# Zero-padded queries, a mask folded into the contraction, and one sliding-window unit per tile in a hybrid attention encoder

## The chip, the cores and the metric

The kernel runs on one core of a Trainium2 chip. The time is the device time of one launch in microseconds, and the figure compared is the median of several runs. The profile shows one execution, instruction by instruction, on the core's engines: TensorE (PE, with its weight loads as PEld), VectorE (DVE), ScalarE (ACT), GpSimd (POOL), and SyncE (SP), which only issues DMAs here.

## The reference

Two layers of a streaming encoder. Each layer normalises its input (1024 prompt frames, and 16 new frames of 8 running streams), projects it, and feeds three groups of heads, all in float32:

```
A  forgetting attention: 4 heads x 64, causal per frame,
   logit[t,s] += sum of log f_j over s < j <= t
B  latent attention: 8 heads, key = 64 columns out of a latent + 32 rotary columns,
   mask: key chunk <= query chunk (chunks of 64 frames)
C  sliding window: 4 query heads on 2 key heads x 64, own chunk and the 2 before,
   a bias by relative position, a learned sink per head
x = x + concat(A, B, C) @ W_out;  x = x + MLP(RMSNorm(x))
```

Each group is softmax(scale * q k^T + bias or mask) v. The mask of B adds -1e30 where the key's chunk lies behind the query's.

## The kernel before

The layer runs in stages: projection of the input, preparation of latents and keys, attention of the prompt, attention of the streams, output projection, MLP. The prompt has 8 tiles of 128 queries. For each tile the work is cut into *units*: the two steps of the latent query's projection (`q1`, `q2`), then units of heads of one kind (`fox`, `swa` for sliding, `mla` for latent). `tile_units` (line 99) decides how many heads share a unit: as many as fit in 1024 score columns, except `swa`, which has two. So a tile has two `swa` units; `mla` has one unit of eight heads in tile 0, two of four in tile 1, four of two in tiles 2 and 3, and eight of one in tiles 4 to 7. The order in a tile is q1, two fox units, q2, the other fox units, the swa units, the mla units; in the last tile the streams' q1 and q2 are put in by position from the end of that list.

All engines walk the same list of units, each with its own lag. For unit i, TensorE transposes the probabilities of unit i-3 (`probs_transposes`, line 2164), computes the scores of unit i (`scores`, lines 2134 and 2136) and the value product of the heads that end with unit i-4 (`values`, line 2187). VectorE copies transposed probabilities of unit i-3 (line 1620), normalises unit i-2 (1629, 1632), takes the maxima of unit i (1657 for mla; 1664 with the bias table for the others) and copies out the heads of i-4 (1681). ScalarE copies its share of the transposed probabilities (1217) and then takes the exponentials of unit i (1234, 1238).

The transposes come in *chunks* of up to four 128 x 128 blocks, each chunk into one of two PSUM banks. Chunks are numbered through the layer: even numbers go to bank 4 and are copied by VectorE, odd ones to bank 5 and are copied by ScalarE.

```
            for g in range(heads):
                h, s0 = h0 + g, score_column(kind, t, g)
                if kind == "fox":
                    rows = slice(64 * (h % 2), 64 * (h % 2) + 64)
                    q, keys, mask = qkTf[rows, h // 2, toks[t]], qkTf[rows, 2 + h // 2, :], cmaskB
                elif kind == "swa":
                    rows = slice(64 * (h // 2), 64 * (h // 2) + 64)
                    q, keys, mask = qkTs[rows, h % 2, toks[t]], qkTs[rows, 2, :], None
                else:
                    q, keys, mask = qTm[t % 2][:, h, :], kTm[:, h, :], mmaskB
```

FoX and sliding heads lie two and two on the 128 partitions, 64 rows each, so their scores contract over 64 rows; a latent head has 96 rows of its own. A score in float32 is two instructions per 512 columns. The masks of fox and mla are added by one more matmul per head, the identity times a bf16 mask, onto the last 128 columns. SP's queue loads, in order, the latent weights, the bias and band tables (line 622 for all loads), and stores new cache entries and finished heads (`mix_d`). GpSimd does nothing during the attention.

Of the kernel before, what the change touches and what calls it, by code (L numbers as in the profile page):

```python
# [21 lines left out]
P = 128  # L22
# [10 lines left out]
QK_M = HD + ROPE  # L33
FF = 4 * D
# [167 lines left out]
def hybrid_step(nc, a, c, o):  # L202

    (y_p, y_s, fk_p, fv_p, lf_p, ckv_p, kr_p, sk_p, sv_p, fk_s, fv_s, lf_s, ckv_s, kr_s, sk_s, sv_s) = o
    with ExitStack() as ctx:
# [35 lines left out]
        mmaskB = keep("mmaskB", [P, P], BF16)  # L241
# [82 lines left out]
        kTm = at("kTm", HT, [QK_M, MLA_H, NPT * P])  # L324
# [14 lines left out]
        qTm = [at(f"qTm{i}", RING + 24576 + i * 4096, [QK_M, MLA_H, P]) for i in range(2)]  # L339
# [4 lines left out]
        triL = at("triL", RING + 48640, [P, P])  # L344

# [37 lines left out]
        constB = at("constB", Z + 512, [P, P])  # L383
# [19 lines left out]
        pro_pe = signal("prologue_pe", 0)  # L403
        pro_dve = signal("prologue_dve", 0)
# [19 lines left out]
        tables_in = signal("wukv_bias_in", 16 * 3)  # L424
# [20 lines left out]
        max_done = signal("max_done", NATTN)  # L445
        has_waited = signal("dve_has_waited", 0)
# [11 lines left out]
        st_prep = signal("stream_rotary_queries", 1)  # L458
        st_rest = signal("stream_queries_and_gates", 1)
# [160 lines left out]
        def _(sp):  # L620
# [4 lines left out]
            for dst, src in ((identF, c["ident"]), (constA, c["cmask"]), (constB, c["mmask"]), (onehot, c["onehot"]),  # L625
# [9 lines left out]
            for l in range(DEPTH):  # L635
# [36 lines left out]
                load(wukv[:].rearrange("p h e d -> p (h e d)"), a["w_ukv"][l], tables_in)  # L672

# [237 lines left out]
        def _(pool):  # L911
# [7 lines left out]
            for l in range(DEPTH):  # L919
# [32 lines left out]
                for t in range(NPT):  # L952
                    if t >= 2:
# [3 lines left out]
                                            ALU.mult).then_inc(lb_ok.sem, 1)  # L957
                for i in range(PC_IN, MLP0):
                    lo(i, i % NSLOT, 1024)
# [107 lines left out]
        def _(act):  # L1067

            act.wait_ge(const_in.sem, 16 * 5)
            nc.scalar.copy(identB[:], identF[:])  # L1070
            nc.scalar.copy(cmaskB[:], constA[:])
            nc.scalar.copy(mmaskB[:], constB[:]).then_inc(pro.sem, 1)
            act.wait_ge(pro_pe.sem, 1)
# [9 lines left out]
            for l in range(DEPTH):  # L1083
# [125 lines left out]
                for i in range(len(UNITS) + LAG):  # L1209
# [8 lines left out]
                    if i < len(UNITS):  # L1218
# [6 lines left out]
                        elif kind == "q2":  # L1225
                            act.wait_ge(sc_mm.sem, sc_mm.at(l, i + 1))
                            nc.scalar.copy(qTm[t % 2][:], S[0:QK_M, :].rearrange("p (h n) -> p h n", h=MLA_H)
# [1360 lines left out]
```

## Time and profile before

| | |
|---|---|
| median of 3 runs | 2941.55 us (2939.71 to 2943.75) |
| the profiled execution | 2936.66 us, its span 2934.9 us |
| mean granted TensorE clock | 0.981 of full speed |
| busy over the span | PE 95%, DVE 61%, ACT 37%, POOL 35% |

The span runs from the first to the last instruction. Busy time of TensorE is modelled from starts, so a busy engine need not be at its peak: what one instruction costs is read from the starts of the next ones.

### The profile page before, as it was taken

The page shows a single profiled execution, that of the slowest core. Times are in us where ns is not written, and L with a number is a line of the kernel's source. Part 1 is how long each engine was busy: PE and PEld are TensorE (multiplying, and loading weights), DVE is VectorE, ACT ScalarE, POOL GpSimd, SP SyncE. Part 2 cuts the span into 40 slices and gives each one's busy share as a digit, 9 for nine tenths or more (in the row PEclk, how much of TensorE's full clock was granted, in tenths as well). Part 3 has the DMA queues.
Part 4 walks back from the last instruction along what each step waited for, and adds up shares of the span by engine and source line. Part 5 has one row for each costly group of instructions (what it writes and reads, how often), then busy time and mean ns, then how long its engine had stood idle before and what let it go on. Part 6 is the DMA issues. An engine that isn't in the chain of part 4 may idle for free.

```text
span 2934.9 us, 40047 instructions
## 1 busy us (share of the span) xinstructions
PE 2787.1 (95%) x15094; PEld 2228.3 (76%) x15094; DVE 1777.0 (61%) x2533; ACT 1076.4 (37%) x1894; POOL 1023.7 (35%) x501
## 2 busy tenths in 40 slices
PE   7999999899999999999999999998899999999995
PEld 5985666678788887888789666667778888788884
DVE  3126777733644649888730477775256564788884
ACT  3224544433332333333332355443243323333333
POOL 2110000012644456777511100000145444567765
PEclk9999999999999999999999989999999999999997
DMA  5210000532334346343131100013323433654331
GB/s 203 62 55 14 23 8 25 156 122 79 126 111 150 142 163 250 131 144 128 59 114 55 47 15 15 16 46 127 129 93 133 150 131 123 256 174 139 129 118 72
DMA packets 164389, 310.68 MB, mean 106 GB/s; under 512 B 24704, under 2 KB 89504, under 8 KB 164256
## 3 DMA queue, kind: packets, MB, share of 16 engines
q1 hardware_dynamic: 159936, 301.82, 29.7%
q10 hardware_dynamic: 4320, 7.08, 0.7%
q8 instruction: 85, 1.39, 0.2%
q14 instruction: 48, 0.39, 0.0%
HBM read 206.42 MB, written 102.44 MB: 105 GB/s over the span
## 4 chain that ended last, share of the span: by engine, by line
PE 84%; DVE 7%; issue 3%; ACT 2%; POOL 2%; DMA 1%; ACTq 0%; SPq 0%; DVEq 0%; POOLq 0%
PE ps L2458 7%; PE ps L2462 7%; PE ps L2460 7%; PE ps L2134 7%; PE ps L2368 7%; PE ps L2369 6%; PE ps L2370 6%; PE ps L1990 5%; PE ps L1988 5%; PE ps L1989 5%; PE ps L2164 4%; PE ps L2187 4%; PE ps L2249 1%; PE ps L2106 1%; PE ps L2318 1%
## 5 line engine op out<-in xcount | busy, mean ns | idle before, releaser
L935 POOL TENSOR_TENSOR w_lo<-w_raw,w_hi 128x1024 fp32r<-128x1024 f32 (+2 forms) x32 | 70.0, 2192 | 1034.3 <-ACT w_hi L1091 1034.3
L2458 PE MATMUL ps<-wq_hi,sa_hi 128*128 128x512 f32 x896 | 350.2, 391 | 5.2 <-DVE x L1921 5.2
L2460 PE MATMUL ps<-wq_lo,sa_hi 128*128 128x512 f32 x896 | 349.8, 390 | 0.0
L2462 PE MATMUL ps<-wq_hi,sa_lo 128*128 128x512 f32 x896 | 349.8, 390 | 0.0
L1921 DVE TENSOR_TENSOR x<-ps,x 128x1024 f32<-128x1024 f32 x224 | 264.2, 1212 | 56.4 <-PE ps L2462 51.7
L1859 DVE TENSOR_TENSOR sa_lo<-ra,sa_hi 128x1024 fp32r<-128x1024 f32 x112 | 280.8, 2509 | 23.9 <-ACT sa_hi L1353 23.9
L975 POOL TENSOR_TENSOR wq_lo<-wsum,wq_hi 128x1024 fp32r<-128x1024 f32 x64 | 157.3, 2459 | 291.0 <-ACT wq_hi L1333 291.0
L1988 PE MATMUL ps<-w_hi,hT_hi 128*128 128x512 f32 (+2 forms) x672 | 248.5, 370 | 0.1
L1990 PE MATMUL ps<-w_hi,hT_lo 128*128 128x512 f32 (+2 forms) x672 | 246.2, 366 | 0.0
L1989 PE MATMUL ps<-w_lo,hT_hi 128*128 128x512 f32 (+2 forms) x672 | 245.1, 365 | 0.0
L1851 DVE TENSOR_TENSOR cq<-ps,cq 128x1024 f32<-128x1024 f32 x48 | 58.7, 1222 | 286.4 <-ACT cq L1394 244.2
L981 POOL TENSOR_TENSOR wq_lo<-bsum,wq_hi 128x1024 fp32r<-128x1024 f32 x64 | 171.2, 2686 | 114.7 <-ACT wq_hi L1344 114.7
L2368 PE MATMUL ps<-hT_hi,wq_hi 128*128 128x512 f32 x512 | 202.1, 395 | 6.8 <-DVE hT_lo L1815 6.8
L981 POOL TENSOR_TENSOR wq_lo<-rq,wq_hi 128x1024 fp32r<-128x1024 f32 x64 | 168.6, 2644 | 96.9 <-ACT wq_hi L1344 96.9
L2458 PEld LDWEIGHTS ps<-wq_hi,sa_hi 128*128 128x128 f32 x896 | 169.0, 189 | 42.0 <-issue 6.0
L2370 PE MATMUL ps<-hT_hi,wq_lo 128*128 128x512 f32 x512 | 200.1, 391 | 0.0
L2369 PE MATMUL ps<-hT_lo,wq_hi 128*128 128x512 f32 x512 | 200.1, 391 | 0.0
L2462 PEld LDWEIGHTS ps<-wq_hi,sa_lo 128*128 128x128 f32 x896 | 168.9, 189 | 35.4
L2460 PEld LDWEIGHTS ps<-wq_lo,sa_hi 128*128 128x128 f32 x896 | 168.9, 189 | 34.6
L975 POOL TENSOR_TENSOR wq_lo<-rq,wq_hi 128x1024 fp32r<-128x1024 f32 x64 | 170.5, 2674 | 57.8 <-ACT wq_hi L1333 57.3
L1394 ACT COPY cq<-ps 128x512 f32<-128x512 f32 x128 | 73.3, 587 | 277.7 <-PE ps L2370 161.3
L2164 PE MATMUL ps<-identF,pbuf 128*128 128x128 f32 x984 | 143.8, 283 | 22.2 <-DVE pbuf L1632 14.3
(317 smaller groups left out, 6377.5 us busy)
## 6 DMA issues: line engine op xcount, KB each, us to landing
ra<-hidden_scratch SPq DMA_DIRECT2D x112, 512.0 KB, 3.3
hidden_scratch<-cq SPq DMA_DIRECT2D x94, 512.0 KB, 2.7
rq<-in_w_up_dram SPq DMA_DIRECT2D x64, 512.0 KB, 3.8
rq<-in_w_down_dram SPq DMA_DIRECT2D x64, 512.0 KB, 4.3
residual_scratch<-x SPq DMA_DIRECT2D x36, 512.0 KB, 5.1
x<-residual_scratch SPq DMA_DIRECT2D x36, 512.0 KB, 6.6
w_raw<-in_w_in_dram SPq DMA_DIRECT2D x16, 512.0 KB, 4.9
mixer_scratch<-omixT SPq DMA_DIRECT2D x16, 512.0 KB, 2.6
```

The lines of the kernel that those rows point to most:

```text
L975: nc.gpsimd.tensor_tensor(wq_lo[o % 4][:], up_source(o)[:], wq_hi[o % 4][:], ALU.subtract).then_inc(up_lo.sem, 1)
L981: nc.gpsimd.tensor_tensor(wq_lo[k][:], down_b_source(o)[:], wq_hi[k][:], ALU.subtract).then_inc(b_lo.sem, 1)
L1859: nc.vector.tensor_tensor(low.rearrange("p k n -> p (k n)"), raws, high.rearrange("p k n -> p (k n)"), ALU.subtract).then_inc(a_lo.sem, 1)
L1988: pe.matmul(out, ah, bh, start=(k == 0), stop=False)
L1989: pe.matmul(out, ah, bl, start=False, stop=False)
L1990: last = pe.matmul(out, al, bh, start=False, stop=(k == n - 1))
L2368: pe.matmul(out, wh[:, cols], h[:, k, :], start=new and k == 0, stop=False, skip_group_check=True)
L2369: pe.matmul(out, wh[:, cols], lo_h[:, k, :], start=False, stop=False, skip_group_check=True)
L2370: last = pe.matmul(out, wl[:, cols], h[:, k, :], start=False, stop=k == 3, skip_group_check=True)
L2458: pe.matmul(out, ah[:, k, :], bh[:, k * 512:(k + 1) * 512], start=new and k == 0, stop=False, skip_group_check=True)
L2460: pe.matmul(out, ah[:, k, :], bl[:, k * 512:(k + 1) * 512], start=False, stop=False, skip_group_check=True)
L2462: last = pe.matmul(out, al[:, k, :], bh[:, k * 512:(k + 1) * 512], start=False, stop=final and k == 1, skip_group_check=True)
```

## The change

The FoX and sliding queries of a tile are copied by GpSimd into buffers of 128 rows (`qzf`, `qzs`), whose other 64 rows hold zeros, and the scores contract over all 128 rows of the keys. The latent mask becomes eight more contraction rows of `qTm` and `kTm`: row b of the keys is 1 where the key lies in the second chunk of block b, row t of the queries is -1e30 for the first chunk's queries of tile t. SP loads these rows, the keys' once and the queries' per tile. The four sliding heads of a tile form one unit. Several prologue semaphores are merged on the way.

```diff
+QK_X = QK_M + 8
 def tile_units(kind, t):
-    n = 2 if kind == "swa" else min(HEADS[kind], 1024 // head_stride(kind, t))
+    n = min(HEADS[kind], 1024 // head_stride(kind, t))
...
+def scores_behind(kind, t):
+    return max(u for u, unit in enumerate(UNITS) if unit[0] == kind and unit[1] == t) + 1
...
-        kTm = at("kTm", HT, [QK_M, MLA_H, NPT * P])
+        kTm = at("kTm", HT, [QK_X, MLA_H, NPT * P])
+        qzf = [at(f"qzf{i}", (RING + 47104, HT + 71296)[i], [P, FOX_H, P]) for i in range(2)]
+        qzs = [at(f"qzs{i}", NRM + 8192 + i * 2048, [P, SWA_H, P]) for i in range(2)]
...
                 load(wukv[:].rearrange("p h e d -> p (h e d)"), a["w_ukv"][l], tables_in)
+                load(kTm[QK_M:QK_X], c["mask_mla_k"].unsqueeze(1).broadcast_to([NPT, MLA_H, NPT * P]), tables_in)
+                def query_mask(t):
+                    load(qTm[t % 2][QK_M:QK_X], c["mask_mla_q"][t].unsqueeze(1).broadcast_to([NPT, MLA_H, P]), qmask_in)
+                query_mask(0)
+                sp.wait_ge(qmask_in.sem, qmask_in.at(l, 16))
+                query_mask(1)
...
                 for t in range(NPT - 1):
                     sp.wait_ge(o_ev.sem, o_ev.at(l, TILE_END[t]))
                     load(mix_d[t], omixT[t % 2][:].rearrange("p k n -> p (k n)"), mix_out[t % 2])
+                    if t + 2 < NPT:
+                        sp.wait_ge(qmask_in.sem, qmask_in.at(l, 16 * (t + 2)))
+                        query_mask(t + 2)
...
+                def pad_zeros(bufs, other):
+                    for buf in bufs:
+                        for r in range(2):
+                            nc.gpsimd.memset(buf[64 * r:64 * r + 64, other(1 - r), :], 0.0)
+                def pad_queries(dst, src, planes, t):
+                    for r in range(2):
+                        rows = slice(64 * r, 64 * r + 64)
+                        last = nc.gpsimd.tensor_copy(dst[t % 2][rows, planes(r), :], src[rows, 0:2, toks[t]])
+                    last.then_inc(qz_ok.sem, 1)
...
+                pool.wait_ge(nb_mm.sem, nb_mm.at(l, NPT))
+                pool.wait_ge(lat_ok.sem, lat_ok.at(l, NT))
+                pad_zeros(qzf, fox_planes)
+                pool.wait_ge(stg_ev.sem, stg_ev.at(l, 2 * NT))
+                pad_queries(qzf, qkTf, fox_planes, 0)
+                pad_queries(qzf, qkTf, fox_planes, 1)
+                pool.wait_ge(lat_ev.sem, lat_ev.at(l, NT))
+                pool.wait_ge(prep_out.sem, prep_out.at(l, 16 * 10))
+                pad_zeros(qzs, swa_planes)
+                pad_queries(qzs, qkTs, swa_planes, 0)
+                pad_queries(qzs, qkTs, swa_planes, 1)
+                for t in range(2, NPT):
+                    pool.wait_ge(sc_mm.sem, sc_mm.at(l, scores_behind("fox", t - 2)))
+                    pad_queries(qzf, qkTf, fox_planes, t)
+                    pool.wait_ge(sc_mm.sem, sc_mm.at(l, scores_behind("swa", t - 2)))
+                    pad_queries(qzs, qkTs, swa_planes, t)
...
                     if kind == "mla" and h0 == 0:
+                        pe.wait_ge(qmask_in.sem, qmask_in.at(l, 16 * (t + 1)))
                         pe.wait_ge(sm_done.sem, sm_done.at(l, UNITS.index(("q2", t, 0, 0)) + 1))
+                    if kind == "fox" and h0 == 0:
+                        pe.wait_ge(qz_ok.sem, qz_ok.at(l, t + 1 if t < 2 else 2 * t + 1))
+                    if kind == "swa" and h0 == 0:
+                        pe.wait_ge(qz_ok.sem, qz_ok.at(l, t + 3 if t < 2 else 2 * t + 2))
...
-                            rows = slice(64 * (h % 2), 64 * (h % 2) + 64)
-                            q, keys, mask = qkTf[rows, h // 2, toks[t]], qkTf[rows, 2 + h // 2, :], cmaskB
+                            q, keys, mask = qzf[t % 2][:, h, :], qkTf[:, 2 + h // 2, :], cmaskB
...
-                            rows = slice(64 * (h // 2), 64 * (h // 2) + 64)
-                            q, keys, mask = qkTs[rows, h % 2, toks[t]], qkTs[rows, 2, :], None
+                            q, keys, mask = qzs[t % 2][:, h, :], qkTs[:, 2, :], None
...
-                            q, keys, mask = qTm[t % 2][:, h, :], kTm[:, h, :], mmaskB
+                            q, keys, mask = qTm[t % 2][:, h, :], kTm[:, h, :], None
```

## Rows read from the trace of the kernel before

**Rows 1.** Stretches of the first attention: us, busy us per engine (instructions), PEclk, DMA share, GB/s.
```profile
342.00:384.20 42.20, 40.69 (x311) 27.92 (x309) 32.60 (x104) 21.47 (x51) 0.00 (x0) 1.00 0.04 14
...
sum 324.00, PE 309.53 PEld 208.61 DVE 234.68 ACT 154.87 POOL 0.00; mean PE 34.39 PEld 23.18 DVE 26.08 ACT 17.21 POOL 0.00
```

**Rows 2.** TensorE's longest waits in the same stage: us, times, longest.
```profile
PE ps L2164 <- DVE pbuf L1632: 7.6, 10, 2.1
```

**Rows 3.** Timeline of TensorE, tile 5: start, us, operation, [idle <-releaser].
```profile
396.82 0.88 PE L2164 MATMUL ps<-identF,pbuf 128*128 128x128 f32 x6
397.63 1.55 PE L2134 MATMUL ps<-qkTf 64*128 64x512 f32 x4
399.12 0.23 PE L2136 MATMUL ps<-cmaskB,identB 128*128 128x128 bf16 x1
...
406.67 0.85 PE L2164 MATMUL ps<-identF,pbuf 128*128 128x128 f32 x6 [0.63 <-ACT ptb L1217]
...
423.80 0.87 PE L2164 MATMUL ps<-identF,pbuf 128*128 128x128 f32 x6
424.51 1.46 PE L2134 MATMUL ps<-kTm,qTm 96*128 96x512 f32 x4
425.80 0.22 PE L2136 MATMUL ps<-mmaskB,identB 128*128 128x128 bf16 x1
425.91 0.88 PE L2164 MATMUL ps<-identF,pbuf 128*128 128x128 f32 x6
```

**Rows 4.** Timeline of TensorE, tile 2, inside a latent unit.
```profile
303.46 0.22 PE L2136 MATMUL ps<-mmaskB,identB 128*128 128x128 bf16 x1
303.51 0.86 PE L2134 MATMUL ps<-kTm,qTm 96*128 96x384 f32 x2
```

**Rows 5.** Groups by line and form, first layer's attention: copies of transposed probabilities.
```profile
L1620 DVE COPY ptb<-ps 128x512 f32<-128x512 f32 x27 | 18.6, 690 | 4.5 <-PE ps L2164 4.3
...
L1620 DVE COPY ptb<-ps 128x256 f32<-128x256 f32 x19 | 8.0, 422 | 2.3 <-PE ps L2164 2.0
...
L1620 DVE COPY ptb<-ps 128x384 f32<-128x384 f32 x12 | 6.7, 557 | 2.4 <-PE ps L2164 2.2
...
L1620 DVE COPY ptb<-ps 128x128 f32<-128x128 f32 x12 | 3.5, 290 | 1.4 <-PE ps L2164 1.2
...
L1217 ACT COPY ptb<-ps 128x512 f32<-128x512 f32 x68 | 39.0, 574 | 3.7 <-PE ps L2164 3.6
```

**Rows 6.** Timeline of VectorE, a latent step of tile 4.
```profile
377.48 0.82 DVE L1657 TENSOR_REDUCE mx<-ps 128x1 f32<-128x640 f32 x1 [0.19 <-PE ps L2136]
```

**Rows 7.** Timeline of VectorE, maxima of a sliding unit, tile 5.
```profile
403.67 0.48 DVE L1664 CUSTOM_DVE_ANT_0 pbuf<-ps,bias,sink_bc 128x256 f32<-128x256 f32 x1
...
404.07 0.48 DVE L1664 CUSTOM_DVE_ANT_0 pbuf<-ps,bias,sink_bc 128x256 f32<-128x256 f32 x1
```

**Rows 8.** Timeline of ScalarE, the same sliding unit and the copy behind it.
```profile
405.47 0.49 ACT L1238 ACTIVATE pbuf<-pbuf,negm 128x256 f32<-128x256 f32 x1
...
405.96 0.56 ACT L1217 COPY ptb<-ps 128x512 f32<-128x512 f32 x1
```

**Rows 9.** Timeline of the preparation: VectorE with GpSimd idle, and beside it.
```profile
205.25 0.34 DVE L1578 SCALAR_TENSOR_TENSOR zc<-zc,lat_rs,gkv_bc 128x128 f32<-128x128 f32 x1
...
213.92 1.16 POOL L955 TENSOR_TENSOR lb<-logf,minus 128x512 f32<-128x512 f32 x1 [0.29 <-PE ps L2073]
214.10 1.12 DVE L1578 SCALAR_TENSOR_TENSOR zc<-zc,lat_rs,gkv_bc 128x128 f32<-128x128 f32 x1
```

**Rows 10.** Timeline of the preparation: the band's load, first key product, bias sum.
```profile
210.71 0.51 SPq L622 DMA_DIRECT2D band<-const_band_dram  x1
...
226.75 7.48 PE L2084 MATMUL ps<-latT,wukv 128*64 128x512 f32 x32 [0.81 <-DVE latT L1588]
...
241.09 1.22 DVE L1608 TENSOR_TENSOR bias<-bias,band 128x1024 f32<-128x1024 f32 x1
```

**Rows 11.** DMA issues from 195 to 245 us: KB, median us to landing.
```profile
band<-const_band_dram SPq DMA_DIRECT2D x1, 128.0 KB, 5.9
```

More of the change, by code:

```diff
@@ L338, in hybrid_step @@
         wukv = at("wukv", RING + 20480, [P, MLA_H, 2, HD])
-        qTm = [at(f"qTm{i}", RING + 24576 + i * 4096, [QK_M, MLA_H, P]) for i in range(2)]
+        qTm = [at(f"qTm{i}", RING + 24576 + i * 4096, [QK_X, MLA_H, P]) for i in range(2)]
         omixT = [at(f"omixT{i}", RING + 32768 + i * 4096, [P, KC, P]) for i in range(2)]
@@ L423, in hybrid_step @@
         gains_in = signal("latent_gains_in", 16 * 4)
-        tables_in = signal("wukv_bias_in", 16 * 3)
+        tables_in = signal("wukv_bias_in", 16 * 4)
+        qmask_in = signal("mla_query_mask_in", 16 * NPT)
         prep_out = signal("prep_out", 16 * 10)
@@ L445, in hybrid_step @@
         max_done = signal("max_done", NATTN)
+        qz_ok = signal("padded_queries_copied", 2 * NPT)
         has_waited = signal("dve_has_waited", 0)
@@ L622, in load @@
                 sp.dma_start(dst, src).then_inc(sem.sem, 16)
-            for dst, src in ((identF, c["ident"]), (constA, c["cmask"]), (constB, c["mmask"]), (onehot, c["onehot"]),
+            for dst, src in ((identF, c["ident"]), (constA, c["cmask"]), (onehot, c["onehot"]),
                              (relb, a["rel_bias"])):
@@ L1067, in _ @@
         def _(act):
-            act.wait_ge(const_in.sem, 16 * 5)
+            act.wait_ge(const_in.sem, 16 * 4)
             nc.scalar.copy(identB[:], identF[:])
-            nc.scalar.copy(cmaskB[:], constA[:])
-            nc.scalar.copy(mmaskB[:], constB[:]).then_inc(pro.sem, 1)
-            act.wait_ge(pro_pe.sem, 1)
+            nc.scalar.copy(cmaskB[:], constA[:]).then_inc(pro.sem, 1)
+            act.wait_ge(pro_tab.sem, 2)
             nc.scalar.mul(skew[:], ps[:, 0:2048].rearrange("p (h n) -> p h n", h=SWA_H)[:, :, 0:384],
@@ L1226, in _ @@
                             act.wait_ge(sc_mm.sem, sc_mm.at(l, i + 1))
-                            nc.scalar.copy(qTm[t % 2][:], S[0:QK_M, :].rearrange("p (h n) -> p h n", h=MLA_H)
+                            nc.scalar.copy(qTm[t % 2][0:QK_M], S[0:QK_M, :].rearrange("p (h n) -> p h n", h=MLA_H)
                                            ).then_inc(sm_done.sem, 1)
@@ L1251, in _ @@
                     if i == 1:
[L1252 removed]
+                        act.wait_ge(st_q.sem, st_q.at(l, 1))
                     if i == FIRST["fox"]:
@@ L1716, in prepare @@
                         if i == 7:
-                            last.then_inc(st_rest.sem, 1)
+                            last.then_inc(st_q.sem, 1)
                 dve.wait_ge(ql_mm.sem, ql_mm.at(l, 1))
@@ L1977, in _ @@
         def _(pe):
-            pe.wait_ge(pro_dve.sem, 1)
+            pe.wait_ge(pro_tab.sem, 1)
             for h in range(SWA_H):
                 last = pe.matmul(bank(h)[:, 0:384], relbb[:, h, :], onehot[:], start=True, stop=True)
-            last.then_inc(pro_pe.sem, 1)
+            last.then_inc(pro_tab.sem, 1)
             pe.wait_ge(pro.sem, 1)
@@ L2540, in shape_constants @@
     tables["cmask"] = np.where(col <= row, f32(0), neg)
-    tables["mmask"] = np.where(col // chunk <= row // chunk, f32(0), neg)
+    block = np.arange(NPT)[:, None]
+    key = np.arange(NPT * P)[None, :]
+    tables["mask_mla_k"] = ((key // P == block) & (key % P >= chunk)).astype(f32)
+    mask_q = np.zeros((NPT, NPT, P), f32)
+    for t in range(NPT):
+        mask_q[t, t, 0:chunk] = neg
+    tables["mask_mla_q"] = mask_q
     lag = (row // chunk + 2) - np.arange(2 * P)[None, :] // chunk
```

23 lines of the change are left out of this document (11 added, 12 removed).

## The prediction

> **What bounds the kernel now.** The change lives in one stage, the prompt attention of each layer, so I read that stage before the whole. The table of stretches [rows 1] is first: in the first layer's attention TensorE is busy 309.53 of 324.0 us, VectorE 234.68, ScalarE 154.87, GpSimd not at all. The reader is to see that two engines are close to full: in the fifth query tile (342 to 384.2 us) VectorE has 32.60 of 42.2 us. The table of waits comes next [rows 2]: TensorE's largest wait on another engine in the whole stage is 7.6 us. So TensorE sets the pace, and a nanosecond taken from it counts until VectorE or ScalarE becomes late.
>
> But "busy" does not say what TensorE is busy with. The timeline of one tile, read by the starts of successive lines, does [rows 3]. From the first of six transposes to the score that follows takes 0.71 us before a latent score with 96 contraction rows (423.80 to 424.51) and 0.81 us before a FoX score with 64 (396.82 to 397.63). Both scores have 768 keys, yet from score to mask it is 1.29 us with 96 rows (424.51 to 425.80) and 1.49 with 64 (397.63 to 399.12). The array pays for going from 128 rows to 64 and back: 0.10 us going in, and 0.20 us for the unhidden second weight load and the way out. Between 96 and 128 rows nothing of the kind appears.
>
> **The change part by part.** Durations are of one profiled execution, 2936.66 us with a span of 2934.9; the median of the runs shown is 2941.55, so 4.9 us go on top at the end.
>
> *FoX queries padded to 128 rows.* Each head's score then costs what the latent one costs. 4 heads, 8 tiles, 2 layers: 64 x (0.10 + 0.20) = 19.2 us off TensorE. The padding itself adds nothing there, since the 96-row score of the same width shows no cost per row.
>
> The rows show the four 64-row passes of a FoX head running one after the other, 1.49 us for what 96 rows do in 1.29. The Trainium skill ("TensorE: Matmul & The Clock Gate", Why this matters for your kernels) says that matmuls of few contraction rows, placed in different row groups, run concurrently; that rule speaks against padding, which occupies the whole array. By the rule up to half of the score time would be within reach of a 64-row kernel; by the rows, this kernel gets none of it, as a mask stands between heads of opposite halves, so nothing is lost.
>
> *Sliding queries padded.* 32 units now enter and leave 64-row mode. I take the same 0.10 going in and 0.10 behind the first pass, and leave out the exit, often followed by another switch: 32 x 0.20 = 6.4 us.
>
> *Four sliding heads as one unit.* One value product of 64 output columns per tile goes, 16 in all. Its two switches are not in the rows; I price them like the FoX ones, 0.10 each: 3.2 us.
>
> *Latent mask as contraction rows.* 8 heads, 8 tiles, 2 layers: 128 mask matmuls go. One costs 0.05 us where another score follows (303.46 to 303.51) [rows 4] and 0.11 where transposes follow (425.80 to 425.91) [rows 3]. I take 0.08: 10.2 us. Eight more rows in the score cost nothing, by the 96-row argument.
>
> Gross sum: 19.2 + 6.4 + 3.2 + 10.2 = 39.0 us.
>
> *What VectorE and ScalarE take back.* Here the diff does something that it does not say. Copies of transposed probabilities go by chunk number, even ones to VectorE, odd ones to ScalarE. The first tile has 1 + 1 + 1 + 2 = 5 chunks before, and 1 + 1 + 2 = 4 after, since the merged sliding unit has 4 blocks in one chunk. Every later unit has two chunks (the sliding pair together two as well), so the parity turns over for the whole rest of the layer. Before, ScalarE had the full chunks (68 of 512 columns) and VectorE the remainders: 12 of 128, 19 of 256 and 12 of 384 columns [rows 5]. After, VectorE gets the full ones: per layer 12 x (0.69 - 0.29) + 18 x (0.69 - 0.42) + 12 x (0.69 - 0.56) = 11.2 us more, in tiles 2, 4, 5 and 6 (one of the 19 is the first tile's). The merged unit gives it back some 0.6 us a tile of small operations.
>
> In the latent steps of those four tiles VectorE has almost no room: in tile 4 it waits 0.19 us for the scores per step [rows 6], and the copy grows by 0.40. So there the mask's gain is void: half of 10.2 = 5.1 us back. In tile 4 the excess is 0.40 - 0.19, say 0.15 us on 8 steps, in tile 2 0.2 us on 4 steps: (1.2 + 0.8) x 2 = 4.0 us back.
>
> The merged unit also makes a longer link. Its maxima take 4 x 0.40 us on VectorE [rows 7], its exponentials 4 x 0.49 us on ScalarE, and only then does ScalarE copy (0.56 us) the transposed chunk that frees the bank [rows 8]: 1.6 + 0.35 + 2.0 + 0.2 + 0.56 = 4.7 us after the scores. TensorE meanwhile has a value block (1.3 us), six transposes (0.7) and a latent score (1.3), 3.3 us. That is up to 1.4 us of stall, and the normalisation of four heads adds one in the next step; before there was a stall of 0.63 us on the same copy [rows 3] and one like it after. I take 0.45 us a tile: 16 x 0.45 = 7.2 us back. For FoX I take back 15%, 2.9 us, for steps that have no value product between two normalisations.
>
> *GpSimd's padding copies.* 16 calls a layer with two copies each; those of tiles 0 and 1 run ahead of the stage, where GpSimd has nothing else to do, and 24 a layer within it, two tiles ahead of their use, so TensorE never waits for them. Behind GpSimd's own waits stand only later copies and the low halves of the output weights, wanted after the stage. What they can do is hold VectorE: an operation with both inputs in SBUF takes 0.34 us with GpSimd idle and 1.12 us while a GpSimd product of 512 columns (1.16 us) runs [rows 9]. Bounds for one copy: 0 if no such operation meets it, 0.55 if it always does (256 columns, half of 1.16). Normalisations are about a quarter of VectorE's time, and half of a delay there should reach the end: 48 x 0.25 x 0.55 x 0.5 = 3.3 us back.
>
> *Loads.* SP's queue now has the key mask, the first query mask and a wait for its landing ahead of the bias and band tables. The band was issued at 210.71 us [rows 10] and took 5.9 us to land [rows 11], so about 216.6; TensorE waits for the tables only at 226.75. A landing plus two more issues shift it by some 4 to 6 us: hidden by 10.1 us. Behind it stand the prep stores, for whose end VectorE waits before the bias sum at 241.09 us [rows 10], and GpSimd before padding the sliding queries; both have over 10 us to spare. Later query masks are issued behind the mixer stores, a tile and more ahead. The dropped constant is far from the path, and in the last tile the first projection of the streams' queries now stands before the last FoX head in place of after it, with two units still between it and its second step. All this I cost at nothing; if the cover failed, each microsecond would show twice, once a layer.
>
> Net: 39.0 - 5.1 - 4.0 - 7.2 - 2.9 - 3.3 = 16.5 us, so 2936.7 - 16.5 = 2920.2 us, and 2925 on the scale of the median. By the bounds alone it lies between 39 us less (2902) and nothing.
>
> **The rivals.** *All of it comes through.* The lags of two to four units absorb the longer sliding unit and VectorE's copies; for it speaks the 27% of VectorE idle over the stage. Gain 30 to 39 us: 2902 to 2911. *VectorE becomes the bound.* The 22.4 us of copies reach the end in full and the merged unit's stall is its full 1 us a tile: 39.0 - 10.2 - 22.4 - 16 + 9 (what VectorE's own idle time and lighter unit cover) is about 0: 2936 to 2946. *GpSimd blocks VectorE, slower.* Every one of the 48 copies holds a normalisation as the row shows, 0.78 us (1.12 - 0.34), at places where VectorE binds: 37 us in place of 3.3, a loss of 17, about 2959. It decides from 19.8 / 48 = 0.41 us a copy on the path. Against it: a copy has half of that row's columns, and VectorE mostly reads PSUM here. The Trainium skill ("SBUF — State Buffer", Who interferes with whom) says that VectorE and GpSimd share a port pair as an exclusive lock, held for the whole instruction, and that scalings like these normalisations can need it too; the row of 1.12 us agrees, for an operation with two SBUF inputs only. *The change doesn't do what it says.* The 0.30 us per FoX head comes from something else than the row count, such as the two sources of the queries, and stays: 39.0 - 19.2 - 6.4 = 13.4 against 5.1 + 4.0 + 7.2 + 3.3 = 19.6 taken back, 6 us slower, about 2948. Against it, the 96-row scores of the same tile.
>
> **How the numbers follow.** My forecast, a net gain of 8 to 27 us (2914 to 2933): 0.56. All through: 0.17. VectorE the bound: 0.14. GpSimd: 0.07. Not as it says: 0.06. 0.2% is 5.9 us, about what a measurement here tells from no change. Faster, below 2935.7: 0.56 + 0.17 and a little of the third, 0.75. Same: most of the third, 0.13. Slower: 0.12. The range leaves out the fastest few and the slower tail: 2904 to 2939; the likeliest case's own is 2914 to 2933.
>
> **What the profile after would show.** FoX and sliding scores with 128 rows, 0.71 us after six transposes, 1.29 us to the mask at 768 keys; no latent mask; VectorE's copies all of 512 columns, ScalarE's the short ones; a longer TensorE wait two or three steps after each sliding unit, behind ScalarE's copy or VectorE's normalisation; GpSimd copies of 256 columns two tiles ahead. I am wrong if TensorE's waits in the stage stay near 10 us a layer (then it is the first rival), if they grow past 30 (the second), or if VectorE's normalisations lengthen during GpSimd's copies (the third).

## The result, and the profile after

The changed kernel takes 2906.72 us (median of 4 runs, 2904.44 to 2910.41); in the same session the kernel before takes 2940.63 (4 runs, 2939.63 to 2943.75). The ratio is 0.9884, 95% interval 0.9867 to 0.9901: some 34 us faster, where 16.5 were forecast. The profiled execution takes 2906.52 us, its span 2904.7, with a mean granted clock of 0.984 (0.981 before). Between the two profiled executions lie 30.1 us, since that of before was 4 us below its median.

The table of stretches of the changed kernel, cut at the tiles of the first layer's prompt attention, is the first view, with columns as in [rows 1]. A tile's length here always runs from the start of the last instruction of the last latent score of one tile to that of the next; the first tile starts with the last product of its `q1`.

```profile
245.22:254.62 9.40, 6.04 (x50) 5.33 (x48) 5.82 (x31) 5.45 (x16) 1.58 (x4) 1.00 0.00 0
254.62:275.16 20.54, 17.64 (x106) 13.31 (x105) 14.48 (x54) 11.08 (x44) 1.58 (x4) 0.92 0.07 27
275.16:303.37 28.21, 25.82 (x191) 17.92 (x190) 24.19 (x80) 15.95 (x52) 1.58 (x4) 1.00 0.06 22
303.37:332.44 29.07, 28.72 (x199) 18.32 (x198) 23.90 (x73) 14.71 (x42) 1.58 (x4) 1.00 0.06 21
332.44:374.57 42.13, 39.77 (x310) 27.96 (x309) 35.39 (x100) 19.77 (x53) 1.58 (x4) 1.00 0.04 15
374.57:417.02 42.45, 40.86 (x304) 28.13 (x302) 35.70 (x94) 18.89 (x49) 1.69 (x4) 1.00 0.04 14
...
sum 274.94, PE 258.23 PEld 177.59 DVE 219.96 ACT 133.24 POOL 9.61; mean PE 32.28 PEld 22.20 DVE 27.49 ACT 16.65 POOL 1.20
```

VectorE has 35.39 of 42.13 us in tile 4, and 35.70 of 42.45 in tile 5. The column to look at next is PEclk: 1.00 in the first tile and 0.92 in the second. The same view of the kernel before, for the first two tiles of the first layer and then of the second:

```profile
244.40:257.04 12.64, 10.20 (x57) 7.87 (x56) 6.62 (x37) 6.57 (x21) 0.00 (x0) 0.85 0.01 1
257.04:280.58 23.54, 22.66 (x133) 15.75 (x133) 16.75 (x65) 12.05 (x47) 0.00 (x0) 0.87 0.06 23
1686.97:1701.01 14.04, 12.87 (x57) 9.97 (x56) 6.69 (x37) 6.57 (x21) 0.00 (x0) 0.61 0.00 0
1701.01:1724.45 23.44, 22.57 (x133) 15.72 (x133) 16.75 (x65) 12.03 (x47) 0.00 (x0) 0.87 0.06 23
```

Before, TensorE was granted 1.2 GHz in place of 2.4 for parts of both tiles, in both layers. [Rows 1] show a stretch at 1.00, and the prediction has no term for the clock.

TensorE's waits in the first layer's attention after the change, largest first:

```profile
PE ps L2218 <- DVE pbuf L1683: 13.7, 19, 2.3
...
PE ps L2218 <- ACT ptb L1268: 0.9, 3, 0.3
```

The wait for VectorE's normalisation grew from 7.6 us [rows 2] to 13.7; that for ScalarE's copy shrank to 0.9, from this in the kernel before:

```profile
PE ps L2164 <- ACT ptb L1217: 3.8, 8, 0.8
```

The groups of copies of transposed probabilities show why (VectorE, then ScalarE):

```profile
L1671 DVE COPY ptb<-ps 128x512 f32<-128x512 f32 x70 | 48.1, 687 | 6.3 <-PE ps L2218 6.0
L1268 ACT COPY ptb<-ps 128x512 f32<-128x512 f32 x28 | 16.2, 578 | 1.7 <-PE ps L2218 1.5
L1268 ACT COPY ptb<-ps 128x256 f32<-128x256 f32 x18 | 6.5, 361 | 1.1 <-PE ps L2218 1.0
L1268 ACT COPY ptb<-ps 128x384 f32<-128x384 f32 x12 | 5.6, 467 | 0.2 <-PE ps L2218 0.2
L1268 ACT COPY ptb<-ps 128x128 f32<-128x128 f32 x12 | 3.1, 254 | 0.7 <-PE ps L2218 0.7
```

Against [rows 5] the engines have changed places, as the prediction read out of the chunk numbers. Last, TensorE's timeline of tile 5, FoX and then the steps behind the merged sliding unit:

```profile
387.37 0.88 PE L2218 MATMUL ps<-identF,pbuf 128*128 128x128 f32 x6
388.08 1.46 PE L2188 MATMUL ps<-qkTf,qzf 128*128 128x512 f32 x4
389.37 0.22 PE L2190 MATMUL ps<-cmaskB,identB 128*128 128x128 bf16 x1
...
397.31 0.66 PE L2218 MATMUL ps<-identF,pbuf 128*128 128x128 f32 x4 [0.22 <-DVE pbuf L1683]
398.26 0.44 PE L2218 MATMUL ps<-identF,pbuf 128*128 128x128 f32 x2 [0.29 <-ACT ptb L1268]
...
400.44 1.09 PE L2218 MATMUL ps<-identF,pbuf 128*128 128x128 f32 x8 [0.45 <-DVE pbuf L1683]
```

A FoX score starts 0.71 us after six transposes and its mask 1.29 us later; in [rows 3] that was 0.81 and 1.49. Behind the sliding unit TensorE waits 0.22 + 0.29 + 0.45 = 0.96 us.

### The profile page after: what moved, and what is told of

The parts are those of the page before. It is cut to its first block, busy times and chain, and to the rows that moved or that the text cites. A ratio compares the mean times of both kernels' runs of the same rounds, so it can differ in the third digit from the quotient of the medians.

```text
span 2904.7 us, 39773 instructions
## 1 busy us (share of the span) xinstructions
PE 2745.5 (95%) x14966; PEld 2216.3 (76%) x14966; DVE 1781.9 (61%) x2451; ACT 1056.3 (36%) x1877; POOL 1054.7 (36%) x581
## 4 chain that ended last, share of the span: by engine, by line
PE 83%; DVE 9%; issue 3%; ACT 2%; POOL 2%; DMA 1%; ACTq 0%; DVEq 0%; SPq 0%; POOLq 0%
PE ps L2512 7%; PE ps L2516 7%; PE ps L2514 7%; PE ps L2422 7%; PE ps L2423 7%; PE ps L2424 7%; PE ps L2041 5%; PE ps L2039 5%; PE ps L2040 5%; PE ps L2188 5%; PE ps L2218 4%; PE ps L2241 3%; PE ps L2303 2%; PE ps L2372 1%; PE ps L2157 1%
```

## The experiments

Every run below is timed in 5 rounds beside the kernel before, whose medians were 2938.89 (first two sessions) and 2939.95 (third). This table has the tile lengths (us) of the first layer in each trace; on the right stand how long TensorE was granted 1.2 GHz in the prompt attention of layer 1 and of layer 2, how long the two attentions are together, and the median. The median belongs to the whole kernel, and the clock also falls in stages that no edit here touches; the column of the attentions leaves those out.

```
tile                    0     1     2     3     4     5     6     7   1.2 GHz   both   median
before              12.64 23.54 28.36 32.66 42.44 43.66 48.43 57.63  10.2 17.1  580.4  2940.6
masks alone         12.54 22.98 27.84 32.32 42.18 43.37 48.13 57.34  13.6 13.6  573.9  2932.7
padding alone       12.42 23.34 27.61 31.39 41.27 42.61 47.18 56.24  10.2  3.4  562.2  2923.1
padding + masks      9.85 22.10 27.24 31.04 41.01 42.32 46.89 55.94   3.4  3.4  553.2  2907.6
 same, parity turned 9.85 21.01 28.09 30.34 41.78 43.03 46.57 55.30   0.0  0.0  552.3  2908.9
merged unit alone    9.93 20.36 28.00 30.59 42.94 43.42 47.44 59.13   6.8  6.8  563.0  2922.9
 same, old parity    9.93 20.98 28.16 31.11 45.29 44.75 49.53 59.79  23.8 20.4  578.5  2935.6
after                9.40 20.54 28.21 29.07 42.13 42.45 46.32 56.82   3.4  3.4  549.8  2906.7
 same, old parity    9.41 20.70 28.39 29.52 42.15 42.84 47.27 58.97   6.8  3.4  556.5  2918.2
 copies x3           9.92 20.97 28.40 29.46 42.36 42.99 46.34 58.17   6.8 13.6  559.3  2914.0
before, filled      13.55 25.34 28.35 32.66 42.44 43.66 48.42 57.63  13.6  3.4  580.2  2936.0
after, filled        9.41 18.93 28.23 29.08 42.14 42.46 46.32 58.09   3.4  3.4  549.3  2904.2
after, some merged   9.40 20.54 28.76 28.63 42.22 42.45 46.32 55.30   3.4  3.4  547.2  2901.5
 some merged, filled 9.40 18.93 28.76 28.62 42.21 42.44 46.32 55.30   0.0  0.0  544.0  2900.6
```

My theory on seeing the result was that the padding's gain came through and that something in tiles 0, 1 and 3 had added to it; the rivals were the clock, the merged unit, and the turned parity.

**Padding alone.** The changed kernel with two sliding units and the latent mask as a matmul.

```diff
-    n = min(HEADS[kind], 1024 // head_stride(kind, t))
+    n = 2 if kind == "swa" else min(HEADS[kind], 1024 // head_stride(kind, t))
-q, keys, mask = qTm[t % 2][:, h, :], kTm[:, h, :], None
+q, keys, mask = qTm[t % 2][:, h, :], kTm[:, h, :], mmaskB
...
```

> The kernel before with the FoX and sliding queries padded to 128 rows alone; latent mask matmuls and two-head sliding units stay, so the chunk parity stays too. Theory A (the gain is the switches between 64 and 128 rows): 64 x 0.30 + 32 x 0.20 = 25.6 us off TensorE, VectorE has room, 20 to 26 us less than before, and the low clock in tiles 0 and 1 stays as before. Theory B (a good part of the measured 34 us is TensorE's clock staying up in tiles 0 and 1, brought by the padding): also the 6.8 and 13.7 us at 1.2 GHz in tile 0 are gone, 26 to 33 us less. Theory C (the 0.30 us do not come from the row count): under 8 us less.

Measured 2923.1 (2920.17 to 2923.98), ratio 0.9946 (0.9932 to 0.9959): 15.8 us faster, less than Theory A's 20 to 26 and B's 26 to 33, and more than Theory C's 8. By the table, tiles 2 to 7 gain 6.88 us, and 6.91 in the second layer: 13.8 / 12 = 1.15 us a tile, 18.4 for sixteen.

**Masks alone.** The changed kernel with two sliding units and the 64-row queries of before.

```diff
-q, keys, mask = qzf[t % 2][:, h, :], qkTf[:, 2 + h // 2, :], cmaskB
+rows = slice(64 * (h % 2), 64 * (h % 2) + 64)
+q, keys, mask = qkTf[rows, h // 2, toks[t]], qkTf[rows, 2 + h // 2, :], cmaskB
...
```

> The kernel before with the latent mask as contraction rows alone. Theory A: 128 x 0.08 = 10.2 us off TensorE and, with the old chunk parity, VectorE can follow: 6 to 10 us less. My prediction's view, that VectorE keeps half of it: 3 to 6 us less. Theory B (clock): more than 10 us less only if tile 0 stays at 2.4 GHz here.

Measured 2932.68 (2930.08 to 2937.55), ratio 0.998 (0.9971 to 0.9989): 6.2 us, where Theory A begins and the prediction's view ends. Tiles 3 to 7 gain 0.26 to 0.34 us each and tile 2 gains 0.52: 2.00 us for 48 heads, 0.04 a head. Theory B's condition didn't come: the stretches at 1.2 GHz are together as long as before.

**Merged unit alone.** The kernel before with one line of the diff. The parity turns over with it.

```diff
-    n = 2 if kind == "swa" else min(HEADS[kind], 1024 // head_stride(kind, t))
+    n = min(HEADS[kind], 1024 // head_stride(kind, t))
```

> The kernel before with four sliding heads in one unit alone, still 64 rows and with the latent mask; the chunk parity turns over. My prediction's terms: 3.2 less for 16 value blocks, 16 x 0.45 = 7.2 more for the longer unit, 4 to 11 more for VectorE's copies of 512 columns: 5 to 15 us slower. The rival, that the merged unit removes waits where it stood instead of adding them (tiles 0, 1 and 3 of the changed kernel are 3 to 5 us shorter each): 5 to 15 us faster. Theory B would show as tile 0 at 2.4 GHz.

Measured 2922.92 (2918.14 to 2925.5), ratio 0.9949 (0.9935 to 0.9962): 16 us faster, a little past the rival's number and far from mine. The part that the prediction charged most to is worth as much alone as the padding. The table shows two places: tiles 0 and 1, where the stretches at 1.2 GHz shrink, and tiles 3 and 6.

**Padding and masks, two sliding units.** The first line of the first diff alone.

> The changed kernel with two-head sliding units again: padding and mask rows, old chunk parity. Theory A: the two parts add, 25.6 + 6 to 10: 28 to 34 us less than before, and the difference to the changed kernel is what the merged unit and the parity are worth together. My prediction's view of the merged unit (7.2 + 4.0 back, 3.2 gained) would put this kernel 5 to 8 us below the changed one; the rival view, that merging helps, puts it 3 to 10 us above.

Measured 2907.6 (2906.57 to 2907.99), ratio 0.9893 (0.9878 to 0.9908): 31.3 us, where the two parts alone give 15.8 + 6.2. Of this surplus of 9.3 us the two attentions hold 2.6 (27.2 us less, where the parts give 18.1 and 6.5): tiles 2 to 7 add up (the masks give 1.86 us on top of the padding, and 2.00 alone), but the first layer's tile 0, which shrank by 0.2 and 0.1 us under each part, shrinks by 2.8 under both together, as the 1.2 GHz stretch in it is gone. The rest lies outside the attention, where the execution with the masks alone has 9.8 us more at 1.2 GHz than the kernel before, and this one 3.4 less. The changed kernel, with the merged unit on top, stands 0.9 us below by the medians, and its attentions are 3.4 us shorter.

**The changed kernel with the old parity.** The first tile's merged unit goes in two chunks of two blocks, so every later chunk keeps its engine of before.

```diff
+def chunk_blocks(u):
+    return 2 if UNITS[u][0] == "swa" and UNITS[u][1] == 0 else 4
-        _chunks += (len(key_blocks(_u)) * UNITS[_u][3] + 3) // 4
+        _chunks += -(-len(key_blocks(_u)) * UNITS[_u][3] // chunk_blocks(_u))
...
```

> The changed kernel, but the first tile's merged sliding unit is cut into two chunks of two blocks, so that the chunk numbers of every later unit have the parity of the kernel before: ScalarE copies the full chunks of 512 columns again, VectorE the short remainders. Theory A (the prediction's: VectorE's 11.2 us of extra copies per layer cost time in the tiles where a VectorE step is tight): tiles 2 and 4, which gained 0.25 and 0.0 us under the change, gain about 1 us each per layer, and the whole is 3 to 6 us faster than the changed kernel. Theory B (parity is worth the same either way, the lags of two to four units absorb it; what counts is the merged unit itself): within 2 us of the changed kernel's 2906.7. Theory C (the merged unit is late in ScalarE's exponentials, and taking copies off ScalarE is what made the merge pay, as in tile 3, which gained 3.7 us): 3 to 8 us slower than the changed kernel, and tile 3 loses about 2 us per layer.

Measured 2918.16 (2912.34 to 2921.01), ratio 0.9927 (0.9915 to 0.994): 11 us slower than the changed kernel. That is Theory C's direction, but past its 3 to 8, and tile 3 loses 0.45 us, not 2. With a merged unit the prediction's price for the parity has the wrong sign. Tile 5 shows the wait: with the old parity TensorE (first row) stands behind ScalarE's copy (second row), which comes after the four exponentials:

```profile
399.62 0.85 PE L2225 MATMUL ps<-identF,pbuf 128*128 128x128 f32 x6 [1.47 <-ACT ptb L1275]
...
398.92 0.56 ACT L1275 COPY ptb<-ps 128x512 f32<-128x512 f32 x1
```

In the changed kernel VectorE copies the full chunk while ScalarE is still at its exponentials, and ScalarE the short one behind them:

```profile
395.86 0.68 DVE L1671 COPY ptb<-ps 128x512 f32<-128x512 f32 x1
...
397.86 0.35 ACT L1268 COPY ptb<-ps 128x256 f32<-128x256 f32 x1
```

TensorE then starts its first four transposes 0.22 us late and waits 0.29 us for the other two, in place of 1.47 for all six. Not all of the 11 us is this wait: the two attentions are 6.7 us longer, and outside them the stretches at 1.2 GHz add up to 103.9 us in this profiled execution, against 83.6 in the changed kernel's.

**The merged unit alone, with the old parity.** The same edit on the kernel before.

> The kernel before with the four sliding heads as one unit and nothing else of the change, but with the first tile's merged unit in two chunks, so that ScalarE keeps the full chunks as before. It stands beside the run with the merged unit alone (2922.9, chunk parity turned over). Theory A (the turned parity, which the prediction priced as a loss of 4.0 us, is a gain, because it takes the 512-column copy off ScalarE just when ScalarE has four exponentials of 0.49 us to do): 5 to 11 us slower than the merged unit alone, 2928 to 2934. Theory B (the prediction's: VectorE's full copies cost, so keeping the old parity is better): 2 to 5 us faster than it, 2918 to 2921. Theory C (in heads of 64 rows the parity makes no difference): within 2 us.

Measured 2935.63 (2928.94 to 2943.23), ratio 0.9987 (0.9978 to 0.9997): 4.3 us faster than the kernel before. Theory A, with 12.7 us a little past its range. With the parity turned the unit alone saved 16.0 us, so about three quarters of that went with the old parity. How much of it is the copy's wait and how much the clock is not separated: the two attentions have 44.2 us at 1.2 GHz, against 13.6 with the parity turned. Its tile 4 shows the cost, on TensorE's timeline and then in the table of stretches:

```profile
362.68 1.30 PE L2171 MATMUL ps<-identF,pbuf 128*128 128x128 f32 x5 [2.46 <-ACT ptb L1224]
```

```profile
355.00:362.00 7.00, 5.22 (x43) 3.45 (x41) 5.87 (x25) 4.41 (x15) 0.00 (x0) 1.00 0.00 1
362.00:369.00 7.00, 6.32 (x20) 4.65 (x21) 3.65 (x12) 3.27 (x8) 0.00 (x0) 0.51 0.01 2
```

A wait of 2.46 us behind ScalarE's copy, and from 362.1 us, within it, the granted clock is 1.2 GHz for 6.8 us. So this stall cost its own length, and the work behind it was slower as well.

**Parity turned, two sliding units.** Padding and masks, with the first tile's FoX unit cut in two chunks.

```diff
+def chunk_blocks(u):
+    return 2 if UNITS[u][0] == "fox" and UNITS[u][1] == 0 else 4
...
```

> The changed kernel with two sliding units of two heads, as in the run with padding and mask (2907.6), but with the first tile's FoX unit in two chunks of two blocks, so that the parity of every later chunk is turned over and VectorE copies the full chunks. Theory A (the turned parity pays only with four sliding exponentials in a row): within 2 us of 2907.6. Theory B (it pays by itself, as ScalarE's share of the copies is the late one in any case): 3 to 6 us faster, 2902 to 2905. Theory C (the prediction's: VectorE is the tight engine in tiles 2, 4, 5 and 6): 2 to 5 us slower, 2910 to 2913.

Measured 2908.9 (2905.59 to 2910.85), ratio 0.9902 (0.9887 to 0.9917): Theory A, 1.3 us from the run without the turn. Inside it two things nearly cancel: tiles 2, 4 and 5 lose 0.85, 0.77 and 0.71 us, and tiles 3, 6 and 7 gain 0.70, 0.32 and 0.64; tile 1 gains 1.1 with the 3.4 us at 1.2 GHz gone.

**GpSimd's copies three times over.** In tiles 2 to 7, so 96 more copies in all.

```diff
-                    for r in range(2):
-                        rows = slice(64 * r, 64 * r + 64)
-                        last = nc.gpsimd.tensor_copy(...)
+                    for j in range(3 if t >= 2 else 1):
+                        if j:
+                            pool.wait_ge(qz_ok.sem, qz_ok.at(l, copied[0]))
+                        for r in range(2): ...
```

> The changed kernel with each of GpSimd's padding copies for tiles 2 to 7 issued three times over: 48 copies become 144 in the attention of the two layers. Theory A (the prediction's price, 0.07 us a copy for holding VectorE): 96 more copies, 6.6 us slower than the changed kernel's 2906.7. Theory B (the copies cost nothing, since VectorE reads PSUM in most of its work and no normalisation lengthened beside a copy): within 1.5 us. The third rival of the prediction (0.78 us a copy): 75 us slower.

Measured 2913.98 (2910.88 to 2915.25), ratio 0.9912 (0.9898 to 0.9926): 7.3 us slower than the changed kernel, 0.076 us a copy; the prediction took 3.3 / 48 = 0.069. The groups of normalisations, in the changed kernel:

```profile
L1683 DVE TENSOR_SCALAR pbuf<-pbuf,rinv 128x768 f32<-128x768 f32 x12 | 7.4, 621 | 0.4
...
L1683 DVE TENSOR_SCALAR pbuf<-pbuf,rinv 128x128 f32<-128x128 f32 x16 | 3.6, 291 | 0.1
```

and with the copies tripled:

```profile
L1689 DVE TENSOR_SCALAR pbuf<-pbuf,rinv 128x768 f32<-128x768 f32 x12 | 7.8, 649 | 0.4
...
L1689 DVE TENSOR_SCALAR pbuf<-pbuf,rinv 128x128 f32<-128x128 f32 x16 | 4.1, 327 | 0.1
```

These two groups lengthen, by 5 and 12%; those of 256, 896 and 1024 columns stay as they were. None comes near the 0.78 us of the third rival. TensorE's one wait for the rotated queries, an operation with two SBUF inputs, grows from 1.7 to 2.1 us. That the total meets Theory A is in part luck, for much of it is clock: these attentions have 20.4 us at 1.2 GHz, 13.6 more than the changed kernel's. Where the clock is the same, in tiles 0 to 5 of the first layer, the 48 more copies cost 2.30 us, 0.048 each.

**The kernel before, with work added.** Identity products where TensorE waits longest in tiles 0 and 1, into the bank that the next transposes fill.

```diff
+                def fill_stall(u):
+                    ch = chunks_of(u)[0][0]
+                    for j in range({1: 2, 5: 2}.get(u, 0)):
+                        if j == 0 and ch >= 2: ...
+                        pe.matmul(bank(4 + ch % 2), identF[:], latT[:, 2, 0:512], start=True, stop=True)
...
+                    fill_stall(u)
                     pe.wait_ge(norm_ok.sem, norm_ok.at(l, n + 1))
```

> The kernel before with nothing of the change, but with work added to TensorE: two identity products of 512 columns in float32 (about 1.7 us by the rows of 512-column scores) where TensorE waits longest in the first two tiles, ahead of the transposes of the first tile's FoX unit and of its latent unit, into the PSUM bank that those transposes then fill; eight products in all. Their results are overwritten. Theory A (a part of the change's gain is the clock: before, TensorE ran at 1.2 GHz for 27 us of tiles 0 and 1 of the two layers, after for 7, because it stood still less often there): the added work keeps the clock up, the stretches at 1.2 GHz shrink to 7 to 14 us, and the kernel is 6 to 10 us faster with more work. Theory B (the clock in these tiles does not set their length, VectorE and ScalarE do): within 2 us of before's 2939. Theory C (the added work adds to the path): 3 to 7 us slower.

Measured 2936.04 (2932.67 to 2942.55), ratio 0.9991 (0.9982 to 0.9999): 2.9 us faster, between the theories; the stretches at 1.2 GHz went from 27.3 to 17.0 us, short of Theory A's 7 to 14, and the two attentions are together as long as before. The first tile in the first layer and in the second shows the two outcomes in one execution:

```profile
246.58:260.13 13.55, 13.22 (x60) 8.85 (x59) 6.70 (x37) 6.57 (x21) 0.00 (x0) 0.75 0.00 1
...
1688.32:1699.09 10.77, 10.24 (x61) 6.99 (x59) 6.62 (x37) 6.57 (x21) 0.00 (x0) 1.00 0.00 0
```

In the second layer the clock holds and the tile takes 10.77 us in place of 14.04; in the first it falls all the same, for 6.8 us of the tile in place of 3.9, and the tile takes 0.9 more. The same instructions of TensorE, 2.8 us apart: that is the price of 6.8 us at 1.2 GHz, and filling this stall doesn't reliably avoid it.

**The changed kernel, filled.** The same with `{4: 2}`, in the stall of 2.4 us (by the starts) ahead of its fall in tile 1.

> The changed kernel with two identity products of 512 columns ahead of the transposes of the first tile's latent unit, where TensorE stands still for 2.4 us (at 261.5 us) just before its clock falls to 1.2 GHz for 3.4 us in tile 1. Four products in all, results overwritten. Theory A (clock): the 3.4 us at 1.2 GHz go in both layers, 2 to 3.5 us faster than the changed kernel's 2906.7. Theory B (VectorE sets the length of this tile): within 1 us. Theory C (the added work delays the transposes): 1 to 3 us slower.

Measured 2904.2 (2900.95 to 2906.18), ratio 0.9878 (0.9863 to 0.9892): 2.5 us below the changed kernel, in Theory A's range, though the intervals of the two ratios overlap. For tile 1 the traces decide more clearly. Changed kernel, TensorE around the stall:

```profile
261.51 0.22 PE L2190 MATMUL ps<-cmaskB,identB 128*128 128x128 bf16 x1
263.94 1.43 PE L2218 MATMUL ps<-identF,pbuf 128*128 128x128 f32 x8 [2.21 <-DVE pbuf L1683]
265.16 1.91 PE L2164 MATMUL ps<-identF,qtok 128*96 128x128 f32 x8
```

and filled, with the stretch of that tile from the table of stretches behind it:

```profile
261.32 1.94 PE L2214 MATMUL ps<-latT,identF 128*128 128x512 f32 x4
263.69 1.09 PE L2227 MATMUL ps<-identF,pbuf 128*128 128x128 f32 x8 [0.44 <-DVE pbuf L1683]
264.62 1.04 PE L2164 MATMUL ps<-identF,qtok 128*96 128x128 f32 x8
```

```profile
254.36:273.29 18.93, 17.79 (x110) 12.77 (x109) 14.62 (x54) 10.96 (x44) 1.67 (x4) 1.00 0.06 24
```

The eight transposes of `qtok` take 1.04 us in place of 1.91, and the tile 18.93 in place of 20.54. But this execution has its 3.4 us at 1.2 GHz in tile 7 instead (58.09 against 56.82), in both layers, and the two attentions together are only 0.5 us shorter.

**Merging where it pays.** The changed kernel with two sliding units in tiles 2, 4 and 7.

```diff
-    n = min(HEADS[kind], 1024 // head_stride(kind, t))
+    n = 2 if kind == "swa" and t in (2, 4, 7) else min(HEADS[kind], 1024 // head_stride(kind, t))
```

> The changed kernel with two sliding units, in place of one, in tiles 2, 4 and 7 alone; the parity stays turned. Against the run with padding and mask, the changed kernel lost 0.97, 1.12 and 0.88 us in these tiles of the first layer, and won in tiles 0, 1, 3 and 6. Theory A (these losses are the merged unit's, its longer link): 4 to 6 us faster than the changed kernel's 2906.7. Theory B (they come from VectorE's full copies, which stay): within 1.5 us of it.

Measured 2901.49 (2900.91 to 2902.2), ratio 0.9874 (0.9859 to 0.9889): 5.2 us below the changed kernel, and all its runs are below all of that; by the ratios, each taken beside the kernel before, it is 2.9, and in the two attentions 2.6. The median is Theory A's, the tiles are not: tile 7 gains 1.52 us, tile 3 0.44, but tiles 2 and 4 are 0.55 and 0.09 us longer. There the merged unit (with the old parity) and VectorE's full copies (with two units) each cost 0.8 to 1.2 us a tile, and together no more than one of them.

**The same, filled.**

> The same with the four identity products ahead of the transposes of the first tile's latent unit, which by themselves made the changed kernel 2.5 us faster. If the two gains are independent: 6 to 8 us faster than the changed kernel's 2906.7, 2899 to 2901. If the tiles' gain moves the clock's falls elsewhere: no faster than the run without them.

Measured 2900.56 (2897.07 to 2903.18), ratio 0.9868 (0.9853 to 0.9883): not separable from the run before it. Tile 1 gains its 1.6 us in both layers and no 1.2 GHz is left in the attentions, which are 3.3 us shorter, while the stretch from there to the MLP has 20.4 us at 1.2 GHz in each layer, against 10.2 and 17.0 without the filling. These two are the fastest versions.

## Why the prediction was off

The time lies in the whole range (2904 to 2939), but where the first rival had it (2902 to 2911, given 0.17) and not in the forecast's own part (2914 to 2933). Attention shrank by 14.42 us in the first layer and 16.20 in the second, 30.6 together, where the net sum was 16.5. The runs take this apart. By tiles 2 to 7, where neither these kernels nor the one before have a stretch at 1.2 GHz, the padding gives 18.4 us over sixteen tiles and the masks on top of it 4.9. With both in, tiles 0 and 1 give 3.9 more than that share, and 20.5 us at 1.2 GHz are gone from them. The merged unit with the turned parity gives the last 3.4. So the first rival's time came in part by luck: of the 35.8 us that it lets come through for padding and masks 23.3 came, and the clock, which it doesn't have, filled in.

**The step that failed** is "What VectorE and ScalarE take back": it charges the turned parity (4.0) and the merged unit's longer link (7.2) side by side, so that with the 3.2 gained for value products the two together lose 8.0. The link was worked out with ScalarE copying a full chunk for 0.56 us behind four exponentials; but the paragraph ahead of it had just moved the full chunks to VectorE. Each price is of the right kind when the other half of the change is absent. The merged unit with the old parity costs 3.3 us in the two attentions (556.5 against 553.2), where 7.2 - 3.2 = 4.0 was charged; by the medians it is 10.6, most of it outside the attention, where that execution has 23.1 us more at 1.2 GHz. The turned parity with two sliding units costs 1.3 us in tiles 2 to 7 of the two layers, and 1.3 by the medians, where 4.0 was charged: tiles 2 and 4 lose 0.85 and 0.77 a layer, for 0.8 and 1.2 in the sum, but tiles 3, 6 and 7 give most of it back. Together the two gain 3.4 us in the attentions and 0.9 by the medians. In tiles 2 to 7 it is the turned parity that lets the merged unit pay: there the unit costs 8.6 us with the old parity (6.8 us of these tiles are at 1.2 GHz) and 0.7 with the turned one. Tiles 0 and 1 gain from it either way, 5.3 and 4.1 us.

**The term that was missing** is the clock. The sum has every duration at the clock of its row. Before, TensorE ran 27.3 us of the two attentions at 1.2 GHz, after 6.8. What this costs is read from the same instructions at either level. Tile 0 of the kernel before takes 12.64 us with 3.9 at 1.2 GHz in the first layer and 14.04 with 10.9 in the second, 0.20 us for each; tiles 0 and 1 with the padding alone take 35.76 with 10.2 and 33.56 with 3.4, 0.32; the filled first tile above gives 0.41, and tile 1 with and without filling 0.47. So the 20.5 us that went are worth 4 to 10, an estimate, and the 3.9 lie at its low end. The clock is not all that tiles 0 and 1 gave. From padding and masks to the changed kernel they gain the 4.1 us above with the same 3.4 us at 1.2 GHz in each layer, and where no 1.2 GHz is left they take 30.86 us with two sliding units (parity turned) and 28.33 with one (some merged, filled). Why the clock falls where it does in tile 0 is not settled: the changed kernel stands still there for longer (1.72 us ahead of the transposes of the rotated queries and 1.64 ahead of those of the FoX unit, where the one before has 0.33 and 2.10) and keeps its clock.

**FoX and sliding padding: right.** 1.29 us to the mask and 0.71 behind the transposes, as forecast. 18.4 us came, where 25.6 less 2.9 and GpSimd's 3.3 make 19.4. The Trainium skill's rule on few contraction rows in different row groups ("TensorE: Matmul & The Clock Gate", Why this matters for your kernels) had nothing to give here: the 64-row passes of [rows 3] ran one after the other, and filling the array with zeros was faster than that. No run has two heads' passes side by side in different row groups, so what the rule would give in another order of the heads stays open.

**Masks: right in sum, by luck.** 4.9 us came (1.86 and 1.84 for six tiles, on top of the padding), 5.1 were forecast net. But it is 0.04 a head in place of 0.08, and it comes in all of tiles 2 to 7, with no tile void, where the prediction had the full price in half of them and nothing in tiles 2, 4, 5 and 6. These runs have the old parity; none shows what the masks are worth with the turned one, for which the prediction voided them.

**GpSimd: the right size, a little high.** 0.048 us a copy where the clock is the same, against 0.069; the third rival falls. The Trainium skill's exclusive lock on a shared port pair ("SBUF — State Buffer", Who interferes with whom) would fit normalisations that lengthen from 291 to 327 ns when there are three times the copies, but no run shows that the lock is the cause; a wait for a whole copy of 0.4 us at every one of them would show far more.

**The second rival** is hardly seen: TensorE's waits for normalisations and copies together rose from 11.4 to 14.6 us, still far from 30 and nearer the 10 that the prediction named as the first rival's sign. **The loads** stayed hidden: the band was issued at 218.36 us, 7.65 later than in [rows 10] and more than the 4 to 6 estimated, and TensorE's first key product at 227.57 still waits for VectorE alone:

```profile
218.36 0.51 SPq L628 DMA_DIRECT2D band<-const_band_dram  x1
```

```profile
227.57 0.65 PE L2135 MATMUL ps<-latT,wukv 128*64 128x512 f32 x2 [0.81 <-DVE latT L1639]
```

## What to carry to other kernels

Price the side effects of a change jointly: a hidden reassignment (here, chunk numbers that decide which engine copies) can remove the very stall that another part of the change is charged with, so redraw the chain after all parts, not after each. Look at the granted clock in the stretches that a change touches before summing durations: here tiles 0 and 1 ran partly at half clock, and part of the gain was that less of it was left. Compare the stage as well as the whole kernel: with the old parity some 5 of the 11 us lay in stages that the edit doesn't touch, beside 20.3 us more at 1.2 GHz there. And an edit need not apply everywhere: the best versions here keep the two units in three tiles, and one of the three, tile 7, brought most of the gain.

## What the runs showed of the hardware

Adding work made the changed kernel no slower (2904.2 us, against 2906.7), and one stretch faster: four matmul instructions put into a stall of 2.4 us took tile 1 from 20.54 to 18.93 us, with PEclk from 0.92 to 1.00. The length of a wait alone does not decide whether the clock falls. In tile 7 TensorE waits 2.3 us between the transposes of the streams' queries and the next ones. The changed kernel keeps 2.4 GHz behind this wait:

```profile
491.06 1.04 PE L2164 MATMUL ps<-identF,qtok 128*96 128x128 f32 x8
494.40 1.09 PE L2218 MATMUL ps<-identF,pbuf 128*128 128x128 f32 x8 [2.31 <-DVE pbuf L1683]
```

The filled one, which comes there 1.8 us earlier, is granted 1.2 GHz from 492.5 to 495.9 us:

```profile
489.24 1.04 PE L2164 MATMUL ps<-identF,qtok 128*96 128x128 f32 x8
492.57 1.97 PE L2227 MATMUL ps<-identF,pbuf 128*128 128x128 f32 x8 [2.30 <-DVE pbuf L1683]
```

So two executions of nearly the same instructions differ by a microsecond or more at such places, and a saving ahead of one can be given back behind it.
